# A transformer kernel on one core: query products of the fourth 128 tokens made during the third chunk's expert turns, with the query weights loaded a second time

## What is computed

```python
qry = (hb @ w_query).reshape(PEER_BLOCK, PEER_HEADS, PEER_KEY_DIM)   # 128 tokens, 8 heads, 256
qry = rms_norm(qry, query_gain)
s1 = einsum("thd,nd->thn", qry[..., :128], sub_keys_1)               # 128 keys a half
s2 = einsum("thd,nd->thn", qry[..., 128:], sub_keys_2)
v1, i1 = top_k(s1, 16); v2, i2 = top_k(s2, 16)
top_s, pos = top_k(all 256 sums of v1 and v2, 16)                    # 16 experts a head
gates = softmax(top_s)
u, vv = expert_down[experts], expert_up[experts]
act = gelu(einsum("thkd,td->thk", u, hb))
out = einsum("thk,thkd->td", gates * act, vv)
```

## Time and profile before

| | us |
|---|---|
| median of three runs | 3313.36 |
| lowest, highest | 3312.57, 3317.35 |
| profiled execution, whole | 3319.61 |
| its span | 3317.7 |

### The profile page before, as it was taken

One profiled execution on the slowest core, in us unless ns is written; L12 is line 12 of the kernel. 1 busy time (PEld: TensorE's weight loads), 2 busy tenths in 40 slices (PEclk: granted clock), 3 DMA queues, 4 the chain that ended last, 5 costly groups with the idle time before them and its releaser, 6 DMA issues.

```text
span 3317.7 us, 36644 instructions
## 1 busy us (share of the span) xinstructions
PE 2938.2 (89%) x12978; PEld 2123.9 (64%) x12978; DVE 2145.4 (65%) x3986; ACT 1419.4 (43%) x2883; POOL 639.5 (19%) x566
## 2 busy tenths in 40 slices
PE   6989999899998899899899988898899777777777
PEld 5868888688876699877798866376567232223222
DVE  7655443487787377355287886875868889555555
ACT  3243222444666344474232336886442433333333
POOL 0000000000111000000002333322443444443442
PEclk8999999999998999999999999899999899999999
DMA  6544444244212378431248999887998899999997
GB/s 248 184 153 127 140 144 143 88 146 141 68 60 85 112 229 267 153 107 40 70 181 345 417 375 386 317 314 259 351 419 354 340 421 421 421 422 422 421 421 331
DMA packets 156917, 833.03 MB, mean 251 GB/s; under 512 B 17344, under 2 KB 19520, under 8 KB 91072
## 3 DMA queue, kind: packets, MB, share of 16 engines
q0 software_dynamic: 73728, 536.90, 40.2%
q1 hardware_dynamic: 79056, 286.30, 25.8%
q10 hardware_dynamic: 3952, 7.48, 0.6%
HBM read 828.52 MB, written 2.10 MB: 250 GB/s over the span
## 4 chain that ended last, share of the span: by engine, by line
PE 58%; DMA 17%; DVE 13%; ACT 8%; issue 3%; POOL 1%; DVEq 0%; SPq 0%; ACTq 0%; POOLq 0%
PE psum L153 57%; DMA tail<-in_experts,tail 17%; ACT L164 3%; DVE tail L187 3%; ACT arena L164 2%; DVE tail L182 2%; ACT tail L164 1%; DVE arena L182 1%; DVE tail L170 1%; DVE region L170 1%; DVE rounded L170 1%; DVE tail L193 1%; ACT region L164 1%; POOL tail L216 1%; PE psum L158 1%
## 5 line engine op out<-in xcount | busy, mean ns | idle before, releaser
L153 PE MATMUL psum<-tail,arena 128*128 128x256 f32 (+2 forms) x4512 | 1427.3, 468 | 223.1 <-ACT arena L164 205.9
L153 PEld LDWEIGHTS psum<-tail,arena 128*128 128x128 f32 x4512 | 844.9, 195 | 760.8 <-issue 672.3
L153 PE MATMUL psum<-rounded,rounded 128*128 128x512 f32 (+1 forms) x5496 | 1110.1, 363 | 40.9 <-DVE rounded L182 24.1
L153 PEld LDWEIGHTS psum<-rounded,rounded 128*128 128x128 f32 x5496 | 929.1, 191 | 202.2 <-issue 30.1
L216 POOL DMA_INDIRECT tail<-in_experts,tail x512 | 582.3, 1137 | 1567.6 <-PE psum L153 744.4
L187 DVE CUSTOM_DVE_ANT_0 tail<-tail 128x1024 f32<-128x1024 f32 x512 | 620.5, 1222 | 287.6 <-DMA tail<-in_experts,tail 286.3
L164 ACT ACTIVATE tail<-tail 128x1 f32<-128x1 f32 (+1 forms) x1056 | 266.5, 252 | 818.6 <-DVE tail L187 785.6
L170 DVE TENSOR_TENSOR rounded<-arena,rounded 128x1024 fp32r<-128x1024 f32 (+2 forms) x272 | 308.7, 1135 | 271.2 <-ACT rounded L164 271.0
L164 ACT ACTIVATE rounded<-arena 128x1024 fp32r<-128x1024 f32 (+3 forms) x304 | 283.9, 950 | 354.6 <-DVE arena L170 150.2
L164 ACT ACT_TABLE_LOAD x220 | 282.3, 1283 | 25.7 <-PE psum L153 19.0
L153 PE MATMUL psum<-arena 128*128 128x1 f32 (+3 forms) x772 | 173.4, 354 | 71.9 <-ACT arena L164 55.6
(11 more groups left out here) (87 smaller groups left out, 1520.2 us busy)
## 6 DMA issues: line engine op xcount, KB each, us to landing
arena<-in_ada SPq DMA_DIRECT2D x136, 512.0 KB, 3.8
arena<-in_fin SPq DMA_DIRECT2D x132, 512.0 KB, 4.6
arena<-in_fout SPq DMA_DIRECT2D x60, 512.0 KB, 4.9
arena<-in_win SPq DMA_DIRECT2D x56, 512.0 KB, 3.7
arena<-in_mxbc SPq DMA_DIRECT2D x32, 512.0 KB, 4.1
arena<-in_pq SPq DMA_DIRECT2D x32, 512.0 KB, 7.8
arena<-in_ain SPq DMA_DIRECT2D x24, 512.0 KB, 4.7
arena<-in_mz SPq DMA_DIRECT2D x16, 512.0 KB, 4.3
```

Of the source, the lines that this page charges most:

```text
L153: return self.e.matmul(o, a, b, start=start, stop=stop, skip_group_check=skip)
```

## The change

The query product of chunk 3 is taken out of the steps that run beside chunk 1's turns and put beside chunk 2's, and so the 16 weight pieces are loaded twice. Chunk 2's product is then made for 128 tokens with two pieces a step, in 12 steps in place of 20; its ranking starts with the fifth of them, turns 201 to 210 for the first 16 ranking steps, and goes on with two in every fourth turn, 213 to 245. Chunk 3's 12 steps are dealt out from turn 262 on, without n % 4 == 3, to turn 277; its ranking takes two steps in each from turn 268 on, then one in every fourth turn.

```diff
-            for kk in range(16):
-                piece(("pq", f, kk), t["pq"][kk])
+            for g in (2, 3) if f else (0,):
+                for kk in range(16):
+                    piece(("pq", g, kk), t["pq"][kk])
...
+        def pe_chunk_pq(e, c):
+            for s in range(12):
+                if s < 8:
+                    key = "pqh", c, s
+                    o = ps.claim(key, QGB)
+                    e.wait_ge(*ps.vacant(key))
+                    for u in range(2):
+                        pe_plain(e, pc["pq", c, 2 * s + u], o[:, part[u]], lambda k: H[:, k, part[c % 2]],
+                                 (lambda k: t_h.at((5, 1, k))) if s == 0 and u == 0 else None)
+                n = s - 2
+                if 0 <= n < 8:
...
+                    for u in range(2):
+                        ins = e.mm(o[:, part[u]], ga["pqh", c, n][:, part[u]], keys[:, u, :])
...
+                    e.mm(ps["qs", c][:, n:n + 1], b[:, part[0]], ones[:, 0:1], True, False)
+                    e.mm(ps["qs", c][:, n:n + 1], b[:, part[1]], ones[:, 0:1], False, True).then_inc(*sq.release(("pqh", c, n)))
+                yield
...
+        def act_chunk_pq(e, c):
+            q = qrs[:, 8 * c:8 * c + 8]
+            for s in range(12):
...
+                if s == 11:
+                    e.wait_ge(*ps.done(("qs", c)))
+                    e.act(q, q, ACT.Ln).then_inc(*ln_ok.tick(("qs", c)))
+                    e.wait_ge(*ln_ok.at(("qs", c)))
+                    e.act(q, q, ACT.Exp, scale=-0.5).then_inc(*q_rs.tick(c))
+                yield
...
+            if f:
+                yield from pe_chunk(e, 2)
+                return
...
+        def pe_chunk(e, c):
+            yield from par(pe_chunk_pq(e, c), pe_tok(e, c))
+
+        def act_chunk(e, c, ranks):
+            yield from par(act_chunk_pq(e, c), act_tok(e, c), both(wait_steps(4), first(ranks, 8, 2)))
+
+        def dve_chunk(e, c, ranks):
+            yield from par(dve_chunk_pq(e, c), both(wait_steps(4), first(ranks, 8, 2)))
...
             elif c < 2 and next(main, True) is None:
                 some(ranks, grp % 2 if n < FIRST_STEPS else 0)
+            elif c == 2 and (n < 262 or n % 4 == 3 or next(main, True) is None):
+                return
             elif grp % 2:
                 some(ranks, 2 if c == 1 else 1)
...
-                    late = pe_tok(e, 3) if c == 2 else iter(())
+                    main = pe_chunk(e, 3) if c == 2 else main
```

More of the change, by code:

```diff
@@ L2192, in dve_wo @@
                 yield
+        def pe_chunk_pq(e, c):
[9 more added lines that the diff above has]
+                if 0 <= n < 8:
+                    key = "sc", c, n
+                    o = ps.claim(key, SCB)
+                    e.wait_ge(*ps.vacant(key))
+                    e.wait_ge(*ps.done(("pqh", c, n)))
+                    for u in range(2):
+                        ins = e.mm(o[:, part[u]], ga["pqh", c, n][:, part[u]], keys[:, u, :])
+                    ins.then_inc(*ga.release(("pqh", c, n)))
+                    if n == 0:
+                        ps.claim(("qs", c), QSB)
+                        e.wait_ge(*ps.vacant(("qs", c)))
+                    e.wait_ge(*sq_ok.at(("pqh", c, n)))
+                    b = sq["pqh", c, n]
+                    e.mm(ps["qs", c][:, n:n + 1], b[:, part[0]], ones[:, 0:1], True, False)
+                    e.mm(ps["qs", c][:, n:n + 1], b[:, part[1]], ones[:, 0:1], False, True).then_inc(*sq.release(("pqh", c, n)))
+                yield
@@ new lines, in act_chunk_pq @@
+        def act_chunk_pq(e, c):
+            q = qrs[:, 8 * c:8 * c + 8]
+            for s in range(12):
+                n = s - 1
+                if 0 <= n < 8:
+                    key = "pqh", c, n
+                    b = sq.claim(key, (0, 1, 2))
+                    e.wait_ge(*sq.vacant(key))
+                    e.wait_ge(*gemm.at(pc["pq", c, 2 * n + 1]))
+                    e.act(b[:, 0:256], ps[key][:, 0:256], ACT.Square).then_inc(*sq_ok.tick(key))
+                    b = ga.claim(key, (0, 1, 2))
+                    e.wait_ge(*ga.vacant(key))
+                    e.act(b[:, 0:256], ps[key][:, 0:256], ACT.Copy).then_inc(*ps.release(key))
+                n = s - 3
+                if 0 <= n < 8:
+                    e.wait_ge(*ga.done(("pqh", c, n)))
+                    e.act(SB[c][:, 256 * n:256 * n + 256], ps["sc", c, n][:, 0:256], ACT.Copy).then_inc(*ps.release(("sc", c, n)))
+                if s == 11:
[4 more added lines that the diff above has]
+                yield
@@ L2196, in pe_pq, with dve_chunk_pq @@
+        def dve_chunk_pq(e, c):
+            for s in range(12):
+                if s == 10:
+                    e.wait_ge(*sq.done(("pqh", c, 7)))
+                    e.ts(qrs[:, 8 * c:8 * c + 8], ps["qs", c][:, 0:8], 1.0 / 256, ALU.mult, EPS,
+                         ALU.add).then_inc(*ps.release(("qs", c)))
+                yield
         def pe_pq(e, f):
@@ L2315, in dve_topk @@
                 for h in (2 * q, 2 * q + 1):
-                    e.wait_ge(*(ps.done(("sc", f, h)) if j else sc_ok.at((c, h))))
+                    e.wait_ge(*(ps.done(("sc", c if f else 0, h)) if j or f else sc_ok.at((c, h))))
                     for a in (2 * h, 2 * h + 1):
@@ L2333, in dve_topk @@
             e.tt(g3, tv, tv[:, :, 0:1].broadcast_to([128, 8, 16]), ALU.subtract).then_inc(*k_dve.tick((c, "above")))
-            e.wait_ge(*q_rs.at(f))
+            e.wait_ge(*q_rs.at(c if f else 0))
             e.wait_ge(*k_dve.at((c, "above")))
@@ L2409, in act_main @@
             yield from act_norm(e, 5, f)
+            if f:
+                yield from act_chunk(e, 2, ranks)
+                return
             yield from par(act_pq(e, f), both(act_tok(e, 2 * f), act_tok(e, 1) if f == 0 else wait_steps(3)),
@@ L2428, in dve_main @@
             yield from dve_norm(e, 5, f)
+            if f:
+                yield from dve_chunk(e, 2, ranks)
+                return
             yield from par(dve_pq(e, f), both(wait_steps(RANK_AT), first(ranks, 14 if f else 12, 2)),
                            both(wait_steps(AGAIN_AT), dve_norm(e, 3, 1) if f == 0 else iter(())))
+        def pe_chunk(e, c):
[4 more added lines that the diff above has]
+            yield from par(dve_chunk_pq(e, c), both(wait_steps(4), first(ranks, 8, 2)))
         RANK_AT, AGAIN_AT = 6, 4
@@ L2623, in pe_experts @@
                     ranks = iter(()) if c == 3 else wait_steps(33)
-                    late = pe_tok(e, 3) if c == 2 else iter(())
+                    main = pe_chunk(e, 3) if c == 2 else main
                 steps_of(c, grp, main, ranks)
-                if grp % 2:
-                    next(late, None)
                 if g:
@@ L2641, in act_experts @@
                     ranks = iter(()) if c == 3 else ranked[c + 1]
-                    late = act_tok(e, 3) if c == 2 else iter(())
+                    main = act_chunk(e, 3, ranked[3]) if c == 2 else main
                 act_gate(e, c, grp)
@@ L2657, in dve_experts @@
                     ranks = iter(()) if c == 3 else ranked[c + 1]
-                    late = wait_steps(3) if c == 2 else iter(())
+                    main = dve_chunk(e, 3, ranked[3]) if c == 2 else main
                 dve_dots(e, c, grp)
```

1 line of the change is left out of this document (added).

## The result

The changed kernel takes **3321.99 us** (median of 16 runs, 3317.54 to 3324.37), the kernel before 3314.33 (16 runs, 3312.57 to 3317.49). The ratio is 1.0021, with an interval of 1.0015 to 1.0028: **5 to 9 us slower**. Run again later, with new runs of the kernel before beside it, the ratio was 1.0018 (1.0009 to 1.0027). I had forecast no change with a gain of 3 us as the likeliest; the range of 3303 to 3327 held the time, the sign was wrong.

A forecast was written before the change was run, and what follows sets the result against it. DMA was taken as the bound, at 420 GB/s from 2640 to 3300 us. Terms +19.9 - 28.9 + 6 = -3.0 us against the median of 3313.4 gave 3310.4 us, called no change; range 3303 to 3327.

The forecast's parts named there:

- Added DMA, +19.9: Loading 16 weight pieces again, 8.39 MB at 421 GB/s, adds 19.9 us of DMA work.
- The hole, -28.9: DMA falls short of 421 GB/s from 2520 to 2640 us, during chunk 2's dense ranking; closing it wholly saves 28.9 us.
- What stays open, +6: Lag from dense ranking in turns 201 to 210 and 268 to 277 leaves 4 and 2 us open; bounds 0 and 13.
- PE, 0; ACT, 0 to 4: PE's narrow product steps cost 0, covered by DMA; ACT's extra table loads at turn 277 cost 0, at most 4 us.
- the two lags don't add: In chunk 3's stretch, DVE's work comes later than PE's and needs only scores, so PE's 16.4 us lag isn't added.
- the second rival: Dense ranking in turns 201 to 210 and 268 to 277 empties the gather queue: +12 us, 3325.5 us; chance 0.24.
- The ring's reach, 17.9 and 20.4 us: Lag of turns behind gather landings that costs nothing: 17.9 us with 11 slots, 20.4 with 12 from turn 260.
- The one of weight loads that bound PE: Weight loads pace the narrow products in turns 196 to 205 and 262 to 272: +22 us, 3335.6 us; chance 0.06.
- The closed hole: The shortfall from 2520 to 2640 us closes wholly, lags within the ring's reach: -9 us, 3304.4 us; chance 0.2.
- The signs I named: If right: 2520 to 2640 mostly above 400 GB/s, DVE under 95% busy, turn 256's gather some 15 us before 2642.
- the place named under "wrong": A new hole around turns 268 to 285, or one around 205 to 215, would show the forecast wrong.

The follow-up runs named there:

- run 2: The changed kernel with chunk 3's weight pieces loaded only by their first 128 of 1024 columns, all instructions kept: 3316.09 us, ratio to before 0.9999.
- run 10: The changed kernel, unchanged, measured and profiled again: 3321.69 us against 3315.99 for the kernel before, ratio 1.0018.
- Run 4: The changed kernel with the odd weight pieces issued from ACT's DMA queue instead of SP's: 3319.52 us, ratio to before 1.0010.
- run 1: The changed kernel with chunk 3's product steps in even turns only (262 to 284), its last 17 ranking steps every fourth turn: 3320.39 us, ratio to before 1.0014.
- run 3: The kernel before with only chunk 2's ranking spread over more turns, no byte or instruction added: 3303.97 us, ratio to before 0.9962.
- runs 8 and 9: The kernel before with spread ranking, product steps from turn 196 in two of three turns (3298.74 us, ratio 0.9947) or three of five (3293.73 us, ratio 0.9935).
- run 7: The changed kernel with chunk 3's ranking taking one step in each of eight product steps in place of two: 3320.97 us, ratio to before 1.0014.

## Why the prediction was right or wrong

- *Added DMA, +19.9.* Right as a term of the sum. 8.39 MB more at a pace that is unchanged behind the holes: the dots of turns 400 and 504 are 4.1 and 4.2 us later than before. As a price it isn't shown: run 2 takes 7.3 MB away and gives back 7 us of 17.4. The 358 GB/s that the Trainium skill names ("DMA: Bandwidth & Descriptors", "Where 436 GB/s comes from") has no part in it; the trace reads 422 from 2900 to 3300 us after the change.
- *The hole, -28.9.* Somewhat too large: 25.7 in the second profile of before. I took one execution's windows for the kernel's, and this one lay 5 us above the median.
- *What stays open, +6.* **This is the term that failed.** It measured 14.3 us in one profile and 11.8 in the other, one past and one just under the bound of 13 I had set. With both means the sum is 19.9 - 27.5 + 13.1 = +5.5 us, inside the measured 5 to 9.
- *Why it failed.* I made the lag of both stretches from DVE's instructions alone, 53.1 and 49.3 us, and put its waits at nothing. They took 60.3 and 55.2 us (60.1 and 55.7 in run 10). The instructions were sized right: without DVE's waits of 8.1 and 6.0 us, 52.2 and 49.2 us are left (of the four own adds in the first, the fourth falls behind turn 211's dots). So the lag grew by 22.8 and 23.9 us in place of 15.6 and 18.0. The turns between, 211 to 245, took 90.0 us where I had said 89.2.
- *Where the waits came from.* PE stood at nothing, "covered by DMA". With its add a step was 3.7 + 0.9 + 1.96 = 6.6 us in my working, against 5.0 of DMA. The duration was right (3.74 for two pieces, 6.45 for a step without waits), the pace was not: a step takes 7.5 us, since the weights get a third of the DMA. I had taken the landing time of 7.8 us from a kernel that asks for one piece a turn and not asked what two a turn would do to it. Run 4 shows the price: with a second queue the first stretch takes 54.0 us, and 6.0 of the 9.0 us of the first hole go. The second hole goes when the steps are not in consecutive turns (run 1).
- *PE, 0; ACT, 0 to 4.* PE was 83% busy in 2500 to 2520 where it was full before, and ACT's three table loads held nobody up: behind them, at 2740.00, ACT itself waits 1.6 us for DVE. But "needs only the scores, so the two lags don't add" was wrong. They add through ACT: own add behind gate, gate behind copy, copy behind PE, 7.0 us in one wait. I had this chain in the second rival and gave it 3.9 us.
- *The ring's reach, 17.9 and 20.4 us.* Right as a way to think, and the two numbers themselves were not tried: with the measured 60.3 and 55.2 us my working leaves 4.9 and 3.5 us open plus what lag there was at the start, where the holes are 9.0 and 4.9. DMA stays at 416 to 419 GB/s all through both product stretches and falls short just after them, when the lag has eaten the queue. That the hole comes behind its cause I had not said.
- *The rivals.* The slower one came true in its place (behind turns 201 to 210 and 268 to 277) and by its mechanism, at about a half of its price: +12 by my working, +7.0 and +6.0 measured. The one of weight loads that bound PE fell (32 records in 3.74 us). The closed hole didn't come.
- *The signs I named.* Of the windows from 2520 to 2640 three read below 400 GB/s, DVE is 97% busy in four of them, and turn 256's gather is issued at 2639.0, 3 us earlier and not 15. The new hole stands right behind turn 277, near the place named under "wrong".
- *Where I looked.* I asked what the change would leave of the hole, not what had made it. DVE's dense ranking was most of it, as I had said (run 3); that product steps in three of four turns held another 8 us I had not. Runs 3, 8 and 9 close 15 to 23 us of it by moving ranking and product steps between turns, at no byte. The split paid 19.9 us for 13 to 16 that were to be had for nothing.

What stays open: how much of the second hole is DVE's ranking pairs and how much the wait for the last sum of squares (run 7 was not clear); what PE's lower granted clock adds to the holes (before the change one add at 2579.10 takes 3.75 us, in place of the 1.96 of the earlier trace rows), since no run sets it apart; and why the profiled executions of the kernel before lie 3 to 5 us above its median where those of runs 8 and 9 don't.

## What to carry to other kernels

In a stage that DMA bounds, write a ledger of two terms, bytes added and shortfall left, and look for what makes the shortfall before paying bytes to close it: work crowded into consecutive turns emptied the ring here, and spreading it over more turns cost no byte and gained 12 to 22 us. When a change asks for transfers twice as fast from a queue that shares the DMA with another, work out the queue's share first, not the landing time of one. A ring hides lag and so moves the hole behind its cause: read the windows after a dense stretch, not those in it.

## What the runs showed of the hardware

- Two queues that both have work got equal numbers of packets, 758 and 753 in 20 us, so with packets of 7.3 and 3.7 KB the bytes went 2:1. A second queue for the short packets raised their part from 33% to 42% with the total at 414 GB/s in place of 417; by then PE didn't wait for weights, so its steps of 6.2 us set what was asked for.
- A 128-column fp32 product with a new weight tile each costs 0.117 us a record (32 in 3.74), against 0.216 for 256 columns: the price went nearly with the columns, and the weight loads, recorded at 191 to 198 ns each, overlapped.
- The granted clock, a mean over each window, fell to 0.66 in the hole after the change (0.71 before), in a window where PE was busy 9.4 of 20 us (11.8 before). It was 1.00 again in 2760 to 2780, where PE was full.
- Two profiles of one program differed by 5.3 us of span with equal medians. Of a difference as small as this case's, a pair of profiles gives the places, and the timed rounds give the sign.
